# Strassen feed-forward: features on the partitions instead of tokens, g rounded in place instead of transposed

## The reference, cut to what matters

```
h2  = rms_norm(x, norm2_gain) * (1 + sc2) + sh2          # 512 x 2048
g   = silu(h2 @ ffn_w_gate) * (h2 @ ffn_w_up)            # 512 x 5632
out = x + g2 * (g @ ffn_w_down)                          # 512 x 2048
```

## Time and profile before

| | us |
|---|---|
| median of 3 runs | 2367.39 (2367.34 to 2368.73) |
| the profiled execution | 2369.26 |
| its span in the profile | 2367.6 |
| first block of the feed-forward, about | 973 to 1063 |
| the ten steps of the loop | 1063.5 to 2302.0 |
| last split and the last down chunks | 2302 to 2367.6 |

### The profile page before, as it was taken

The page is one execution under the profiler, slowest core; times in us unless marked ns, Lnnn a source line. Parts: engine busy times, 40 slices in busy tenths (PEclk is TensorE's granted clock), DMA queues, the critical chain, the costliest instruction groups (busy, mean ns, idle before and its releaser), DMA issues.

```text
span 2367.6 us, 28777 instructions
## 1 busy us (share of the span) xinstructions
PE 2317.0 (98%) x10544; PEld 1868.4 (79%) x10544; DVE 1640.9 (69%) x2057; ACT 832.5 (35%) x1147; POOL 82.5 (3%) x80
## 2 busy tenths in 40 slices
PE   6999999999999999999999999999999999999998
PEld 5877787788876788788878787878787878887877
DVE  5976876587757433666777777776868686868683
ACT  4233324343236322343333333333424242424232
POOL 0012100021001000000000000000000000000000
PEclk8999999999999999999999999999999999999999
DMA  9976681677640143234444445353445353545452
GB/s 341 321 263 222 238 306 61 230 237 262 205 145 19 53 161 98 86 110 143 162 134 156 159 151 166 126 179 129 161 133 186 124 180 122 166 142 170 138 164 81
DMA packets 233745, 392.36 MB, mean 166 GB/s; under 512 B 16441, under 2 KB 108063, under 8 KB 232520
## 3 DMA queue, kind: packets, MB, share of 16 engines
q1 hardware_dynamic: 233672, 391.39, 49.8%
HBM read 382.93 MB, written 11.03 MB: 166 GB/s over the span
## 4 chain that ended last, share of the span: by engine, by line
PE 85%; DVE 7%; issue 3%; ACT 2%; DMA 2%; SPq 1%; DVEq 0%; ACTq 0%
PE PS L1057 11%; PE PS L1059 10%; PE PS L1058 10%; PE PS L1112 7%; PE PS L1114 7%; PE PS L1113 7%; PE PS L676 6%; PE PS L678 6%; PE PS L677 6%; PE PS L840 2%; PE PS L683 2%; PE PS L684 2%; PE PS L685 2%; PE PS L816 2%; DVE acc_first L1611 1%
## 5 line engine op out<-in xcount | busy, mean ns | idle before, releaser
L1452 ACT ACTIVATE whi<-stage 128x1024 fp32r<-128x1024 f32 x368 | 390.7, 1062 | 840.6 <-PE PS L1059 444.8
L2000 DVE TENSOR_TENSOR wlo<-stage,whi 128x1024 fp32r<-128x1024 f32 x368 | 449.8, 1224 | 181.0 <-ACT whi L1452 181.0
L1057 PE MATMUL PS<-whi,xc_hi 128*128 128x512 f32 x1216 | 480.8, 395 | 3.2 <-DVE g_tok L2102 2.2
L1059 PE MATMUL PS<-whi,xc_lo 128*128 128x512 f32 x1216 | 474.7, 390 | 0.0
L1058 PE MATMUL PS<-wlo,xc_hi 128*128 128x512 f32 x1216 | 474.3, 390 | 0.0
L1560 DVE TENSOR_TENSOR wlo<-stage,whi 128x1024 fp32r<-128x1024 f32 x136 | 173.1, 1274 | 217.8 <-ACT whi L1230 217.7
L676 PE MATMUL PS<-hhi,whi 128*128 128x512 f32 x768 | 311.3, 405 | 7.5 <-DVE wlo L1560 4.6
L678 PE MATMUL PS<-hhi,wlo 128*128 128x512 f32 x768 | 303.0, 395 | 0.0
L677 PE MATMUL PS<-hlo,whi 128*128 128x512 f32 x768 | 302.8, 394 | 0.0
L1230 ACT ACTIVATE whi<-stage 128x1024 fp32r<-128x1024 f32 x136 | 144.2, 1062 | 437.9 <-PE PS L678 308.6
L1057 PEld LDWEIGHTS PS<-whi,xc_hi 128*128 128x128 f32 x1216 | 228.1, 188 | 77.4 <-DVE wlo L2000 7.5
(11 more groups left out here) (297 smaller groups left out, 2481.7 us busy)
## 6 DMA issues: line engine op xcount, KB each, us to landing
stage<-in_ffn_w_up SPq DMA_DIRECT2D x168, 512.0 KB, 4.0
ada_ring<-in_ada_w SPq DMA_DIRECT2D x128, 512.0 KB, 4.9
stage<-in_ffn_w_gate SPq DMA_DIRECT2D x128, 512.0 KB, 3.7
stage<-in_ffn_w_down SPq DMA_DIRECT2D x88, 512.0 KB, 4.6
stage<-in_w_in SPq DMA_DIRECT2D x80, 512.0 KB, 6.1
ada_first<-in_ada_w SPq DMA_DIRECT2D x64, 512.0 KB, 6.7
stage<-in_w_out SPq DMA_DIRECT2D x32, 512.0 KB, 3.7
xnat<-in_x SPq DMA_DIRECT2D x4, 1024.0 KB, 8.0
```

Source lines behind the costliest of these rows:

```text
L1057: mm(PS[:, b, :], x_hi, w, start=start, stop=False)
L1059: return mm(PS[:, b, :], x_lo, w, start=False, stop=stop)
L1452: f(whi[:, p % NW, :, :].rearrange("p k n -> p (k n)"), slot_of(p), ACT.Copy).then_inc(w_hi, 1)
L2000: v.tensor_tensor(wlo[:, p % NW, :, :].rearrange("p k n -> p (k n)"), slot_of(p), whi[:, p % NW, :, :].rearrange("p k n -> p (k n)").bitca ...
```

## The change

The feed-forward's products are turned round. The weights (128 x 128 out of a chunk) are the stationary operand, and 256 tokens of x are the moving one. `half_tiles` takes the place of `split_tile`: per bank and k-slice it makes 2 x 3 matmuls of 256 columns where there were 3 of 512. Everything that follows keeps its number of instructions and its shapes, but a tile now has features on the partitions: tile t of `g_tok` holds token half t // 2 and features of column pair t % 2. The transposes of g are gone, in the loop and behind it. ScalarE rounds `g_tok` itself into `f_hi` (in the place of `s11` and `u_sb`, which change places), and VectorE writes `f_lo` over `g_tok`. The waits of `f_high` are on `g_ready` instead of the transposes. In the queues, the first two `f_high` and `f_low` stand ahead of chunk 9's `hi_at` and `lo_at`, the others ahead of chunk 10's. A down chunk keeps its 24 matmuls of 512 columns; its moving operand is now two runs of 256. Behind the loop 14 unread products stand in one row, with a wait for one bank.

```diff
-        f_hl = [at(f"f_hl{b}", [P, 2, 2, S], F32R, offset) for b, offset in enumerate((RM, RH + 114688))]
+        f_hi = at("f_hi", [P, 4, S], F32R, RM)
+        f_lo = at("f_lo", [P, 4, S], F32R, RH + 114688)
...
-            def split_tile(b, x_hi, x_lo, w, w_l, start, stop):
-                mm(PS[:, b, :], x_hi, w, start=start, stop=False)
-                mm(PS[:, b, :], x_hi, w_l, start=False, stop=False)
-                return mm(PS[:, b, :], x_lo, w, start=False, stop=stop)
+            def half_tiles(b, c, kk, x_hi, x_lo, start, stop):
+                for i in range(2):
+                    o = PS[:, b, HT * i:HT * (i + 1)]
+                    cols = slice(P * (2 * (b % 2) + i), P * (2 * (b % 2) + i + 1))
+                    mm(o, whi[:, c % NW, kk, cols], x_hi, start=start and i == 0, stop=False)
+                    mm(o, wlo[:, c % NW, kk, cols], x_hi, start=False, stop=False)
+                    last = mm(o, whi[:, c % NW, kk, cols], x_lo, start=False, stop=stop and i == 1)
+                return last
...
-                    if p == SET1[1][2]:
-                        for b in range(2):
-                            pe.wait_ge(bank_free[WB + b], w_free(n))
-                        g_transposes(n, 0, WB)
-                    if p == SET1[2][2]:
-                        pe.wait_ge(g_lo, 4 * n + 2)
-                        g_transposes(n, 1, WB)
...
-            for half in range(2):
-                unread_products(WB, 6 if half == 0 else 9, x_any)
-                pe.wait_ge(g_ready, 4 * n + 2 * half + 2)
-                ...
-            unread_products(WB, 7, x_any)
+            pe.wait_ge(bank_free[PB], p_base + 2 * n)
+            unread_products(PB, 14, xc_hi[:, 0, 0:2, :].rearrange("p q n -> p (q n)"))
...
-                    act.wait_ge(gt_pe, 4 * n + (i + 1 if i < 2 else 4))
-                    f(f_of(i)[0], PS[:, bank0 + i % 2, :], ACT.Copy).then_inc(g_hi, 1)
+                    act.wait_ge(g_ready, 4 * n + order.index(i) + 1)
+                    f(f_hi[:, i, :], g_tok[:, i, :], ACT.Copy).then_inc(g_hi, 1)
...
             def from_nine(n):           # VectorE
-                lo_at(n, 9)
-                f_low(n, range(2))
-                lo_at(n, 10)
-                f_low(n, range(2, 4))
+                f_low(n, LOWER_FIRST[:2], LOWER_FIRST)
+                lo_at(n, 9)
+                f_low(n, LOWER_FIRST[2:], LOWER_FIRST)
+                lo_at(n, 10)
```

More of the change, by code:

```diff
@@ L400, in f_of @@
         def f_of(f):
-            return f_hl[f // 2][:, f % 2, 0, :], f_hl[f // 2][:, f % 2, 1, :]
+            return (w[:, :, :].rearrange("p (h b) (c n) -> p h b c n", h=2, c=2)[:, :, f // 2, f % 2, :]
+                    for w in (f_hi, f_lo))
         x1_sqt = at("x1_sqt", [P, 4, S], F32, RQ + 32768)
@@ L1073, in _ @@
                             if q == A21:
-                                xh, xl = x21_hi[:, kp % 4, cols], x21_lo[:, kp % 4, cols]
+                                xh, xl = x21_hi[:, kp % 4, :], x21_lo[:, kp % 4, :]
                             else:
-                                xh, xl = xc_hi[:, kp, q, cols], xc_lo[:, kp, q, cols]
-                            last = split_tile(4 * m + t, xh, xl, whi[:, c % NW, kk, :], wlo[:, c % NW, kk, :],
-                                              kp == 0 and kk == 0, kp == GCH - 1 and kk == 1)
+                                xh, xl = xc_hi[:, kp, q, :], xc_lo[:, kp, q, :]
+                            last = half_tiles(4 * m + t, c, kk, xh, xl, kp == 0 and kk == 0,
+                                              kp == GCH - 1 and kk == 1)
                     last.then_inc(w_used, 1)
@@ L1094, in product @@
                     for kk in range(CK):
-                        cols = slice(P * t, P * (t + 1))
-                        last = split_tile(bank0 + t, xc_hi[:, CK * j + kk, q, cols], xc_lo[:, CK * j + kk, q, cols],
-                                          whi[:, p % NW, kk, :], wlo[:, p % NW, kk, :],
+                        last = half_tiles(bank0 + t, p, kk, xc_hi[:, CK * j + kk, q, :], xc_lo[:, CK * j + kk, q, :],
                                           j == 0 and kk == 0, j == 3 and kk == 1)
@@ L1111, in down @@
                         fh, fl_ = f_of(f)
-                        mm(PS[:, WB + d, :], wh[:, cols], fh, start=f == 0, stop=False)
-                        mm(PS[:, WB + d, :], wh[:, cols], fl_, start=False, stop=False)
-                        last = mm(PS[:, WB + d, :], wl[:, cols], fh, start=False, stop=f == 3)
+                        o = PS[:, WB + d, :].rearrange("p (h n) -> p h n", h=2)
+                        mm(o, wh[:, cols], fh, start=f == 0, stop=False)
+                        mm(o, wh[:, cols], fl_, start=False, stop=False)
+                        last = mm(o, wl[:, cols], fh, start=False, stop=f == 3)
                     if d == 0:
@@ L1119, in down @@
                 last.then_inc(w_used, 1)
[L1121 to L1128, removed]
             pe.wait_ge(xs_lo, GCH)
@@ L1452, in hi_at, with f_high @@
                 f(whi[:, p % NW, :, :].rearrange("p k n -> p (k n)"), slot_of(p), ACT.Copy).then_inc(w_hi, 1)
-            def f_high(n, fs, bank0=WB):
-                for i in fs:
-                    act.wait_ge(gt_pe, 4 * n + (i + 1 if i < 2 else 4))
-                    f(f_of(i)[0], PS[:, bank0 + i % 2, :], ACT.Copy).then_inc(g_hi, 1)
+            def f_high(n, tiles, order):
+                for i in tiles:
+                    act.wait_ge(g_ready, 4 * n + order.index(i) + 1)
+                    f(f_hi[:, i, :], g_tok[:, i, :], ACT.Copy).then_inc(g_hi, 1)
             def m1_out(n):
@@ L1476, in from_nine @@
             def from_nine(n):
+                f_high(n, LOWER_FIRST[:2], LOWER_FIRST)
                 hi_at(n, 9)
[L1478 to L1481, removed]
+                f_high(n, LOWER_FIRST[2:], LOWER_FIRST)
+                for p in range(10, NPOS):
                     hi_at(n, p)
@@ L1508, in _ @@
             n = NFB - 1
-            f_high(n, range(2), 0)
-            f_high(n, range(2, 4), 4)
+            f_high(n, UPPER_FIRST, UPPER_FIRST)
             def copy_out(part, tiles=range(ST)):
@@ L2036, in _, with f_low @@
             p_base, r_base = uses(16) + 1, uses(15) + 1
[L2038 to L2042, removed]
+            def f_low(n, tiles, order):
+                for i in tiles:
+                    dve.wait_ge(g_hi, 4 * n + order.index(i) + 1)
+                    v.tensor_tensor(f_lo[:, i, :], g_tok[:, i, :], f_hi[:, i, :].bitcast(F32), ALU.subtract
+                                    ).then_inc(g_lo, 1)
             def down_out(n, e, p, ds=range(2)):
@@ L2227, in _ @@
             n = NFB - 1
-            f_low(n, range(2), 0)
-            f_low(n, range(2, 4), 4)
+            f_low(n, UPPER_FIRST, UPPER_FIRST)
             for e in range(GCH):
```

8 lines of the change are left out of this document (4 added, 4 removed).

## The result

| | before | after |
|---|---|---|
| median, us | 2368.06 (2367.34 to 2368.77, 4 runs) | 2431.88 (2430.88 to 2433.48, 4 runs) |
| span of the profiled execution | 2367.6 | 2431.8 |
| granted clock over the span | 0.993 | 0.984 |
| ratio, 95% interval | | 1.027 (1.0252 to 1.0288) |

The change makes the kernel slower by 64 us. Slower was the forecast's direction, and 2431.88 lies in its range, but 27 us above the time that I named.

The account below looks back on a forecast made before the run. TensorE was taken to bound the kernel: the number of matmuls times the cost of each, plus its waits. From 2369.26 us profiled, +45.6 - 9.9 + 2.4 = +38.1 gave 2407.4, so a median of 2405 us; range 2345 to 2440.

Parts of the forecast that it names:

- The halves: Product matmuls: 3744 of 512 columns become 7488 of 256; 3420 count in the time, +45.6 us at 120 ns a half.
- (a): Product matmuls: the 13.3 ns surplus is paid once in each, so a half costs 120 ns; +45.6 us, chance 0.43.
- The proportional surplus: Rival for the product matmuls: surplus grows with the columns, a half costs 113.3 ns; matmul term 0, 2360 us, chance 0.23.
- the floor: Rival for the product matmuls: only the weight load holds the pace, 110 ns a half; -22.8 us, 2337 us, chance 0.12.
- the hand-over: Rival for the product matmuls: each starts after load and stream, about 125 ns a half; +79.8 us, 2440 us, chance 0.22.
- The transposes: In the feed-forward loop: of 27 us of transposes in ten steps, removing them gives back only 9.9 us.
- the first group: First eight transposes of a step, before chunk 8: removal saves 0 in nine steps, as chunk 8 awaits its lo part.
- the second group: Second group of transposes in a step: removal saves 0.88 us in each of nine steps, 7.9 us.
- Rival 4: Loop transposes: chunk 8 starts earlier and all 27 us come back; 2388 us at 120 ns a half, no separate chance given.
- Behind the loop: Tail: TensorE idles 6.3 us, then some twelve down matmuls run at 1.2 GHz; +2.4 us (0 to 3.2).
- (c): Product matmuls: hand-over only after load and stream, about 125 ns a half; +79.8 us, 2440 us, chance 0.22 with above.

Follow-up runs that it names:

- f3: The kernel before plus seven dense rows of 48 unread fp32r matmuls, 64 to 512 columns wide, behind the last transposes: 2417.85 us (one run, more work).
- e1: The changed kernel with TensorE's loop over the ten steps written out, no branch back: 2393.97 us, 1.0102 of before.
- f4: The changed kernel with 40 unread products behind the loop instead of 14: 2429.44 us (one run).
- g3: The kernel before with each product matmul cut into two of 256 columns, loop and transposes kept, tokens stationary: 2433.04 us, 1.0291 of before.
- e2: The kernel before with two steps in the body of TensorE's loop, 2244 instructions and four branches back: 2373.61 us, 1.0023 of before.

## Why the prediction was right, and where it was off

**The halves: right mechanism, a size too high.** Predicted 3420 x 13.3 = +45.6 us. A half is 120.0 ns, as (a) has it. But a whole in the loop cost 228.3 ns, not the 226.7 of the earlier trace rows: the base was taken from the quiet tail, although the prediction's first paragraph has 228.7 for the loop. So 3420 x 11.7 = 40 us. The proportional surplus, the floor and the hand-over fall by the kernel's row and by f3.

**The exposed loads: a term left out.** In the loop of before some starts lie 0.03 to 0.27 us further apart than in a dense row, apart from the transposes and the waits, most of them by 0.1 us at the first matmuls of a chunk. They add up to 7.0 us, and in e1's loop to 1.7: -5.3. That they are weight loads which nothing hides is my reading of them.

**The instruction fetch: a term that was left out.** This is what the account had wrong. The prediction doubled the number of matmuls and priced only what each costs in a dense row, not the program that they are in. The loop's body grew past what TensorE keeps, and e1 puts its price at 37.9 us. From the rows: 26.8 us of gaps, 15.8 at the lower clock and in exposed loads behind them, less 4.1 for nine waits at chunk 1 that they cover, is 38.5.

**The transposes: right.** Chunk 8 waits 1.49 us in nine steps (1.7 predicted) for the lo part that the first group had run in the shadow of, nothing waits before chunk 10, and only the second group and step 0 gave their time back: -9.9. Rival 4, all 27 us back, falls.

**Behind the loop: right.** Predicted: downs 9.8 us after the last product and a dozen matmuls at 427 ns, +2.4. Measured: 9.4, ten matmuls, +2.0; f4 takes them away.

**The sum.** In spans of the profiles e1 is 25.0 us over before, and its stages come to that: 1.7 less ahead of the feed-forward, 5.0 for the first block and chunk 0 (396 x 13.3 = 5.3 by my terms), 19.8 for the loop (3024 x 11.7 = 35.4, less 7.9 and 2.0 for the transposes and 5.3 for the loads, is 20.2), 2.0 for the tail. Of the predicted 38.1 that is 13 less. The branch then adds 39 in the same measure (2431.8 - 2392.6). So 2405 was two errors of opposite sign, one left out of the sum altogether. That 2431.88 fell into the range was luck: its upper end was set by (c), and (c) is not what happened. By its own terms, without the branch, the prediction would have been 11 us too high (2405 against e1's 2393.97).

**Open.** Why about two blocks more than the body are fetched at a branch, why the packet starts 0.3 us later against the last matmul in the changed kernel than in g3, and why the clock fell behind eight gaps there and behind four in g3. Nor was the threshold between 1100 and 1738 instructions narrowed. Shifting the transposes of before by a chunk, the one idea that these runs leave for its wait of 0.65 us, was not tried.

## What to carry to other kernels

When an edit splits instructions, count the program too: compare the instruction queue's packets with the size of the program, and at each branch back look for an idle stretch put down to "issue", or to an operand that had long been ready. A smaller moving operand pays a fixed cost more often and gains nothing below the floor (112 ns here). Before removing work that fills a wait, ask what that wait is for; here half of the transposes were free.

## What the hardware showed that I had not expected

- An fp32r matmul costs its columns at 2.4 GHz plus 11 to 15.5 ns, once, at 256 to 512 columns, and no less than 112 ns at 64 and at 192.
- A loop's body of 1738 or 2244 instructions on TensorE was fetched again whole at each branch (about 9 and 11 packets), one of 1100 was not. A branch cost 1.9 (e2) to 3.0 us (changed kernel) on the average, and in the changed kernel 14 to 28 matmuls at half the clock behind eight of the nine.
- A GpSimd product stretched VectorE's operations beside it from 1.22 to 2.0 and 2.3 us.
- The granted clock stood at 0.52 in a dense row of matmuls of 128 columns, behind one of 64 columns at the full clock, with TensorE busy all the time.
- After a fetched block had arrived TensorE's next matmul took 1.5 to 1.8 us to start, in 22 gaps of three kernels.
